# New byte offsets for the FFN hidden tiles and for the mixers' view of the normed activations in an fp32 two-part matmul kernel

## The reference, cut to what matters

```python
# first block, each of 2 layers; second block alike, with three attention branches and no cross attention
h = h + 0.5 * swiglu_ffn(rms_norm(h, ffn1_norm[l]), ffn1_w_in[l], ffn1_w_out[l])   # up 1024 -> 2 x 2816, down 2816 -> 1024
h = h + hybrid_mixer(rms_norm(h, mix_norm[l]), w_in[l], ..., w_out[l])
h = h + memory_cross_attention(rms_norm(h, xattn_norm[l]), rms_norm(mem, mem_norm[l]), w_q, w_kv, w_o)
h = h + 0.5 * swiglu_ffn(rms_norm(h, ffn2_norm[l]), ffn2_w_in[l], ffn2_w_out[l])

def swiglu(h, w_in, w_out):
    g, u = split(h @ w_in, 2)
    return (silu(g) * u) @ w_out
```

## Time and profile before

| what | value |
|---|---|
| median of 3 runs | 2719.12 us (2718.63, 2719.12, 2724.09) |
| the profiled execution | 2723.83 us |
| its span, first to last instruction | 2721.8 us |
| instructions in the profile | 39409 |
| TensorE matmul busy | 2666.2 us, 98% of the span |
| VectorE, ScalarE, GpSimd busy | 56%, 50%, 9% |
| mean granted TensorE clock | 0.990 |
| HBM traffic | 156 GB/s over the span |

### The profile page before, as it was taken

One profiled execution on the slowest core, in us unless ns is written; L12 is line 12 of the kernel. 1 busy time (PEld: TensorE's weight loads), 2 busy tenths in 40 slices (PEclk: granted clock), 3 DMA queues, 4 the chain that ended last, 5 costly groups with the idle time before them and its releaser, 6 DMA issues.

```text
span 2721.8 us, 39409 instructions
## 1 busy us (share of the span) xinstructions
PE 2666.2 (98%) x14932; PEld 2275.9 (84%) x14932; DVE 1525.2 (56%) x2103; ACT 1365.0 (50%) x2147; POOL 256.3 (9%) x155
## 2 busy tenths in 40 slices
PE   8999999999999999999999999999999999999998
PEld 6889987888888898787888879888888888878887
DVE  5557635465555774455555546467555555557654
ACT  5447335454544562555445445555445444455543
POOL 0100201000000002200100000443000000245000
PEclk9999998999999999999999999999999999999999
DMA  6555213355555541146855554325555555324654
GB/s 246 186 178 172 90 47 102 131 183 185 197 185 187 169 147 48 62 155 161 214 186 182 186 187 151 108 94 173 188 184 183 185 186 169 125 92 136 201 186 136
DMA packets 117803, 427.54 MB, mean 157 GB/s; under 512 B 13004, under 2 KB 14796, under 8 KB 117132
## 3 DMA queue, kind: packets, MB, share of 16 engines
q1 hardware_dynamic: 117152, 424.59, 47.8%
q10 hardware_dynamic: 492, 0.69, 0.1%
HBM read 423.79 MB, written 1.44 MB: 156 GB/s over the span
## 4 chain that ended last, share of the span: by engine, by line
PE 92%; DVE 3%; ACT 3%; issue 1%; DMA 1%; POOL 0%; SPq 0%; ACTq 0%; DVEq 0%
PE bank L460 75%; PE bank L1621 2%; PE bank L964 2%; PE bank L480 2%; PE bank L656 1%; PE bank L1668 1%; PE bank L1637 1%; PE bank L602 1%; PE bank L1124 1%; PE bank L1135 1%; ACT hi_slots L434 1%; PE bank L1133 1%; DVE lo_slots L448 1%; DMA raw<-w_full 1%; PE bank L1651 0%
## 5 line engine op out<-in xcount | busy, mean ns | idle before, releaser
L448 DVE TENSOR_TENSOR lo_slots<-raw,hi_slots 128x1024 fp32r<-128x1024 f32 x732 | 899.6, 1234 | 770.1 <-ACT hi_slots L434 769.6
L434 ACT ACTIVATE hi_slots<-raw 128x1024 fp32r<-128x1024 f32 x788 | 830.1, 1057 | 671.1 <-PE bank L460 660.2
L460 PE MATMUL bank<-hi_slots,x_hi 128*128 128x512 f32 x1600 | 634.3, 396 | 4.4 <-DVE lo_slots L425 4.0
L460 PE MATMUL bank<-hi_slots,x_lo 128*128 128x512 f32 x1600 | 624.2, 390 | 0.0
L460 PE MATMUL bank<-lo_slots,x_hi 128*128 128x512 f32 x1600 | 623.6, 390 | 0.0
L460 PEld LDWEIGHTS bank<-hi_slots,x_hi 128*128 128x128 f32 x1600 | 301.1, 188 | 66.9 <-DVE lo_slots L425 4.8
L460 PEld LDWEIGHTS bank<-hi_slots,x_lo 128*128 128x128 f32 x1600 | 300.8, 188 | 64.0
L460 PEld LDWEIGHTS bank<-lo_slots,x_hi 128*128 128x128 f32 x1600 | 301.3, 188 | 59.0
L460 PE MATMUL bank<-x_hi,hi_slots 128*128 128x256 f32 x1152 | 332.2, 288 | 1.3 <-ACT bias_mem L975 0.8
L460 PE MATMUL bank<-x_lo,hi_slots 128*128 128x256 f32 x1152 | 326.1, 283 | 0.0
L460 PE MATMUL bank<-x_hi,lo_slots 128*128 128x256 f32 x1152 | 326.0, 283 | 0.0
(11 more groups left out here) (310 smaller groups left out, 3070.4 us busy)
## 6 DMA issues: line engine op xcount, KB each, us to landing
raw<-w_full SPq DMA_DIRECT2D x792, 512.0 KB, 3.3
bias_mem<-bias_rows SPq DMA_DIRECT2D x8, 288.0 KB, 7.2
mem<-mem_t SPq DMA_DIRECT2D x2, 1024.0 KB, 7.8
const<-consts SPq DMA_DIRECT2D x1, 1664.0 KB, 7.1
h<-x_t SPq DMA_DIRECT2D x1, 1024.0 KB, 5.2
final<-finals SPq DMA_DIRECT2D x2, 512.0 KB, 7.3
out_t<-h SPq DMA_DIRECT2D x4, 256.0 KB, 2.3
bias_rows<-junk ACTq DMA_DIRECT2D x1, 384.0 KB
```

The lines of the kernel that those rows point to most:

```text
L434: nc.scalar.activation(w_hi[s], raw[s][:, :], ACT.Copy).then_inc(hi_ready[s], 1)
L448: nc.vector.tensor_tensor(w_lo[s], raw[s][:, :], w_hi[s].bitcast(F32), ALU.subtract).then_inc(lo_ready[s], 1)
L460: mm = nc.tensor.matmul(out, lhsT=a, rhs=b, start=start and n == 0, stop=stop and n == len(passes) - 1)
```

## The change

`x_hi` and `x_lo` become rooms that are 16 floats (64 bytes) longer. Each room has two views: `x_hi`/`x_lo` begin 64 bytes in, `xm_hi`/`xm_lo` at its start. Where the normed activations are for a mixer or the cross attention, ScalarE and VectorE write them through the `xm` views and TensorE reads them through these; FFNs and output projections keep `x_hi`/`x_lo`. `hid_pad` shrinks from 32 to 16 floats. `param`, `small`, `seam_gain`, `junk` and the pads are put in another order. Worked out as above, the starts modulo 2048 after the change are: `hi_slots`, `lo_slots`, `h` 128 as before; `x_hi`, `x_lo` 128 as before, though at other addresses (`x_hi` from byte 59520 to 77952, `x_lo` from 67712 to 100480); `xm_hi`, `xm_lo` 64; `hid_hi`, `hid_lo`, `hid`, `xs` 128 instead of 192; `const` 128 instead of 64; `mem_hi`, `mem_lo`, `y_hi`, `y_lo` 64 as before. The number of instructions, their order and their waits stay.

```diff
+SHIFT = 16
         h = sb("h", [P, TT, D_MODEL])
-        x_hi = sb("x_hi", [P, KT, TOK], F32R)
-        x_lo = sb("x_lo", [P, KT, TOK], F32R)
-        junk = sb("junk", [P, HALF])
-        mem_pad = sb("mem_pad", [P, 496])
+        param = sb("param", [P, N_PARAM])
+        small = sb("small", [P, 16])
...
+        mem_pad = sb("mem_pad", [P, 24])
...
+        x_hi_room = sb("x_hi_room", [P, KT * TOK + SHIFT], F32R)
         const = sb("const", [P, N_CONST])
-        param = sb("param", [P, N_PARAM])
         ab_now_hi = sb("ab_now_hi", [P, KT * 8], F32R)
+        x_pad = sb("x_pad", [P, 48])
+        x_lo_room = sb("x_lo_room", [P, KT * TOK + SHIFT], F32R)
+        x_hi, x_lo = (room[:, SHIFT:].rearrange("p (k t) -> p k t", k=KT) for room in (x_hi_room, x_lo_room))
+        xm_hi, xm_lo = (room[:, 0:KT * TOK].rearrange("p (k t) -> p k t", k=KT) for room in (x_hi_room, x_lo_room))
...
-        hid_pad = sb("hid_pad", [P, 32], F32, ffn_mem)
+        hid_pad = sb("hid_pad", [P, SHIFT], F32, ffn_mem)
         hid_hi = sb("hid_hi", [P, FT, TOK], F32R, ffn_mem)
...
-        def act_turned(normed, hf, banks, gain):
+        def act_turned(normed, hf, banks, gain, to=x_hi):
...
-                nc.scalar.activation(x_hi[:, k, :], turned(banks, k), ACT.Copy,
+                nc.scalar.activation(to[:, k, :], turned(banks, k), ACT.Copy,
...
-            pe_lead(E, group, ev, x_hi, x_lo, lambda k: pe.wait_ge(*x_ready(normed, k)), rest)
+            pe_lead(E, group, ev, xm_hi, xm_lo, lambda k: pe.wait_ge(*x_ready(normed, k)), rest)
...
-            feature_block(u % SLOTS, x_hi, x_lo, bank[2 + g % 2][:, 0:TOK]).then_inc(block_done[u % SLOTS], 1)
+            feature_block(u % SLOTS, xm_hi, xm_lo, bank[2 + g % 2][:, 0:TOK]).then_inc(block_done[u % SLOTS], 1)
...
```

More of the change, by code:

```diff
@@ L250, in build @@
         h = sb("h", [P, TT, D_MODEL])
-        x_hi = sb("x_hi", [P, KT, TOK], F32R)
-        x_lo = sb("x_lo", [P, KT, TOK], F32R)
-        junk = sb("junk", [P, HALF])
-        mem_pad = sb("mem_pad", [P, 496])
+        param = sb("param", [P, N_PARAM])
+        small = sb("small", [P, 16])
+        eps_col, mean_part = small[:, 0:4], small[:, 8:8 + TT]
+        squares = small[:, 4:8].rearrange("p (a t) -> p a t", a=2)
+        rstd, rstd_first = small[:, 10:10 + TT], small[:, 12:12 + TT]
+        seam_gain = sb("seam_gain", [P, KT])
+        mem_pad = sb("mem_pad", [P, 24])
         raw_mem = ExitStack()
@@ L273, in build @@
         mem_sum, mem_rstd = (bias_mem[:, at_norm + n * TOK:at_norm + (n + 1) * TOK] for n in range(2))
[L274 to L279, removed]
+        junk = sb("junk", [P, HALF])
+        stage_pad = sb("stage_pad", [P, 432])
         ffn_mem, mix1, cross, mix2 = ExitStack(), ExitStack(), ExitStack(), ExitStack()
-        hid_pad = sb("hid_pad", [P, 32], F32, ffn_mem)
+        hid_pad = sb("hid_pad", [P, SHIFT], F32, ffn_mem)
         hid_hi = sb("hid_hi", [P, FT, TOK], F32R, ffn_mem)
@@ L621, in pe_turn_scaled, with dve_turned @@
                         mm.then_inc(sems["xt_ps"], 1)
-        def act_turned(normed, hf, banks, gain):
+        def act_turned(normed, hf, banks, gain, to=x_hi):
             for k in range(4 * hf, 4 * hf + 4):
                 act.wait_ge(sems["xt_ps"], normed * 4 + k // 2 + 1)
-                nc.scalar.activation(x_hi[:, k, :], turned(banks, k), ACT.Copy,
+                nc.scalar.activation(to[:, k, :], turned(banks, k), ACT.Copy,
                                      scale=gain[:, k:k + 1]).then_inc(sems["xhi_ready"], 1)
-        def dve_turned(normed, hf, banks, gain, part=(0, 4)):
+        def dve_turned(normed, hf, banks, gain, part=(0, 4), to=(x_hi, x_lo)):
             for k in range(4 * hf + part[0], 4 * hf + part[1]):
                 dve.wait_ge(sems["xhi_ready"], normed * KT + (k | 1) + 1)
-                nc.vector.scalar_tensor_tensor(out=x_lo[:, k, :], in0=turned(banks, k), scalar=gain[:, k:k + 1],
-                                               in1=x_hi[:, k, :].bitcast(F32), op0=ALU.mult,
+                nc.vector.scalar_tensor_tensor(out=to[1][:, k, :], in0=turned(banks, k), scalar=gain[:, k:k + 1],
+                                               in1=to[0][:, k, :].bitcast(F32), op0=ALU.mult,
                                                op1=ALU.subtract).then_inc(sems["xlo_ready"], 1)
@@ L896, in pe_mix1_project @@
             pe.wait_ge(sems["ab_lo"], E.after("ab_lo", 1))
-            three(bank[4][0:8, 0:TOK], [(ab_now_hi[:, k * 8:k * 8 + 8], ab_now_lo[:, k * 8:k * 8 + 8], x_hi[:, k, :],
-                                         x_lo[:, k, :]) for k in range(KT)]).then_inc(sems["ab_ps"], 1)
-            pe_section(E, 1, 1, 3, x_hi, x_lo)
+            three(bank[4][0:8, 0:TOK], [(ab_now_hi[:, k * 8:k * 8 + 8], ab_now_lo[:, k * 8:k * 8 + 8], xm_hi[:, k, :],
+                                         xm_lo[:, k, :]) for k in range(KT)]).then_inc(sems["ab_ps"], 1)
+            pe_section(E, 1, 1, 3, xm_hi, xm_lo)
         def act_mix1_project(E):
@@ L1054, in pe_gdn @@
         def pe_gdn(E):
-            pe_group(E, 4, 4, 0, x_hi, x_lo)
+            pe_group(E, 4, 4, 0, xm_hi, xm_lo)
             pe.wait_ge(sems["ab_sb"], E.after("ab_sb", 1))
@@ L1066, in pe_gdn @@
             mm.then_inc(sems["gdn_ss"], 1)
-            pe_group(E, 5, 5, 0, x_hi, x_lo)
+            pe_group(E, 5, 5, 0, xm_hi, xm_lo)
             for i in range(4):
@@ L1081, in pe_gdn @@
                 mm.then_inc(sems["gdn_bc"], 1)
-            pe_token_pair(E, 6, 6, 0, x_hi, x_lo)
+            pe_token_pair(E, 6, 6, 0, xm_hi, xm_lo)
             pe.wait_ge(sems["gate_dve"], E.after("gate_dve", 4))
@@ L1108, in pe_gdn @@
                 pe_gate_rows(G_BETA, t, bank[4], c("ident")).then_inc(sems["row_ps"], 1)
-                pe_token_pair(E, 6, 6, 2, x_hi, x_lo, (t,), [bank[2][:, tile_cut(n)] for n in range(TT)])
+                pe_token_pair(E, 6, 6, 2, xm_hi, xm_lo, (t,), [bank[2][:, tile_cut(n)] for n in range(TT)])
                 pe.wait_ge(sems["kv_scaled"], E.after("kv_scaled", 3 * t + 3))
@@ L1802, in pe_cross @@
             pe_normed(E, 2, 13, 7, lambda: pe.wait_ge(sems["mem_ev"], E.after("mem_ev", MEM_EVACS)))
-            pe_section(E, 14, 8, 1, x_hi, x_lo)
+            pe_section(E, 14, 8, 1, xm_hi, xm_lo)
             for s in range(SLOTS):
@@ L1825, in pe_mix2_project @@
                 for s in range(2 if g in (1, 4) else SLOTS):
-                    pe_block(E, E.mid(g, s), s, g, x_hi, x_lo)
+                    pe_block(E, E.mid(g, s), s, g, xm_hi, xm_lo)
                 if g in (1, 4):
-                    pe_token_pair(E, g, g, 2, x_hi, x_lo)
+                    pe_token_pair(E, g, g, 2, xm_hi, xm_lo)
                 if g == 2:
@@ L2054, in act_full @@
             for hf in range(2):
-                act_turned(normed, hf, turns, gain)
+                act_turned(normed, hf, turns, gain, xm_hi)
         def dve_full(E, n, state, normed, turns, gain):
@@ L2059, in dve_full @@
             for hf in range(2):
-                dve_turned(normed, hf, turns, gain)
+                dve_turned(normed, hf, turns, gain, to=(xm_hi, xm_lo))
         def act_ffn_ended(E, state, u):
@@ L2215, in _ @@
                         for hf in range(2):
-                            act_turned(E.normed(1), hf, FFN_TURNS, gain(E, "mix", 0, KT))
+                            act_turned(E.normed(1), hf, FFN_TURNS, gain(E, "mix", 0, KT), xm_hi)
                         act_mem_key(E, 1)
@@ L2240, in _ @@
                         for hf in range(2):
-                            act_turned(E.normed(2), hf, STICK_TURNS, p1(E, "xattn", 0, KT))
+                            act_turned(E.normed(2), hf, STICK_TURNS, p1(E, "xattn", 0, KT), xm_hi)
                         act_mem_values(E, 3)
@@ L2323, in _ @@
                         split_lo(E, FFN_UNITS - 1)
-                        dve_turned(E.normed(1), 0, FFN_TURNS, gain(E, "mix", 0, KT))
+                        dve_turned(E.normed(1), 0, FFN_TURNS, gain(E, "mix", 0, KT), to=(xm_hi, xm_lo))
                         dve_mem_unit(E, 0)
-                        dve_turned(E.normed(1), 1, FFN_TURNS, gain(E, "mix", 0, KT))
+                        dve_turned(E.normed(1), 1, FFN_TURNS, gain(E, "mix", 0, KT), to=(xm_hi, xm_lo))
                         dve_mem_unit(E, 1)
@@ L2344, in _ @@
                         for hf in range(2):
-                            dve_turned(E.normed(2), hf, STICK_TURNS, p1(E, "xattn", 0, KT))
+                            dve_turned(E.normed(2), hf, STICK_TURNS, p1(E, "xattn", 0, KT), to=(xm_hi, xm_lo))
                         for j in range(2, MEM_KEPT):
```

## The result

| | median | runs |
|---|---|---|
| before | 2718.88 us | 4 (2718.21 to 2724.09) |
| changed | 2695.18 us | 4 (2693.01 to 2700.3) |

The ratio is 0.9911, 95% interval 0.9893 to 0.993: 24 us faster. The forecast of 2689 is a ratio of 0.989; it lies just outside the first interval and inside the second, and both medians lie in the range.

What follows compares the result with a forecast made beforehand. TensorE, busy 98% of the span, was taken to bound the kernel through the distance between matmul starts. The gains, 13.3 + 17.6 + 0.8 - 1.7 = 30.0 us, off the 2719.1 us median gave 2689, range 2678 to 2704.

Steps and rivals of the forecast that it cites:

- (1): FFN down half: hid moved from 192 to 128 cuts 233.4 to 227.1 ns over 2112 matmuls, 13.3 us gained.
- (2): Mixers: x streamed from 64 goes from 120 to a mean 114.9 ns over 3456 matmuls, 17.6 us gained.
- A: Rival: all streamed x blocks settle at the longer distance, 118.0 ns; 19.8 us gained, 2699 us; chance 0.15.
- B: Rival: all streamed x blocks settle at the shorter distance, 113.3 ns; 37.0 us gained, 2682 us; chance 0.17.
- (3): token_pair, stationary operand now at 64: 120.0 to 117.9 ns over 376 matmuls, 0.8 us gained.
- (4): Transposes, with const, hid and xs moved to 128: costed at nothing, with up to 4.9 us either way.
- (5): Given back through late operands in the delta rule's part, token pairs and half-clock starts: 1.7 us in all.
- The cover: In the projection, weight reload and split (5.6 us) were to finish before the slot's next use (10.9 to 11.3 us).
- Rival C: Only one edit works, or late VectorE or ScalarE takes back about half of (2): 2698 to 2706 us; chance 0.08.
- D: Rival: the two distances belong to the stages, not the tiles, so nothing changes, 2719 us; chance 0.03.
- E: Rival: coarser address bits matter, so moved x_hi and x_lo slow the FFN's up half; 17 us slower, 2736; chance 0.03.

Runs made afterwards that it cites:

- kernel of the mixers alone: The changed kernel with the hid pad back at 32 floats (hid at 192, mixers' x streamed from 64): 2706.99 us, ratio 0.994 to the kernel before.
- e9_restarts: The changed kernel with const back at 64 modulo 256, the small tile hid at 192, ab_now_hi shifted too: 2694.14 us, ratio 0.9892 to the kernel before.

## Why the prediction was right

The direction, the mechanism and the range held, and the steps, each by its own measure, are:

- **(1) `hid`:** 13.3 us foreseen, 13.8 measured in the traces, 11.8 as a time by itself. The up half was the right row to take it from.
- **(2) `x` streamed:** 17.6 foreseen with the mix of the `y` blocks (114.9 ns), 18.3 measured (114.6). 2413 of some 3400 steps in the trace are at the short distance, close to the 8 in 12 of `y`. The two distances were foreseen rightly; that the mix came so near was luck. Six of the eight short `y` blocks are one unbroken run, and in the changed kernel it fell into the long distance, which left 3 in 12 short. With `x` at the same offset the mean was 115.3 in the kernel of the mixers alone and 115.6 in e9_restarts. Rivals A and B, all blocks at one distance, didn't come: long streams took the short one, every other gate the long one.
- **(3) token pair:** 0.8 foreseen, 1.4 measured. 138 of some 370 steps were at the short distance, which L964, the row it was taken from, shows in 22 of 351.
- **(4) `const` and the transposes at nothing:** this step failed. The streams behind the transposes got slower: 2.1 us in the up half, 1.1 us in the `y` blocks, and both went back when e9_restarts moved `const` and `hid` back. I had looked at the length of the transposes and not at what follows them. The 5 us that I had set beside (4) covered it in size.
- **(5) given back:** 1.7 us foreseen, 3.9 in new waits. The cover failed at one place, the first mixer's projection (a wait for `lo_slots`, 1.6 us); and where attention begins TensorE waits another 2.3 us, because a small VectorE operation now falls behind the start of a GpSimd one; the forecast had no term for that. The cover was reckoned with 5.6 us for a reload and its split, from the median landing of 3.3 us and without other work in between. At the place of the wait it took 14.9 us, more than the 10.9 to 11.3 us after which a slot is used again.

So the parts came to 33.5 us where 31.7 was foreseen, and 7.1 was lost where 1.7 was: 26 in place of 30. The wait of TensorE for a split is the one that the forecast said should not appear.

One reading of the forecast was too short. It says that the mean duration doesn't show the difference, from the first of three forms (396 ns for either tile). The other two forms had 390 ns with `x` and 394 with `hid`, and with `hid` at 128 its three have 391, 389 and 389. The durations hint at the effect, and give less than its size.

Rival C (one edit without effect) fell with the two single edits, D (nothing to do with the tiles) with `hid` at ten offsets and the FFN's `x` at 64. E asked for coarser address bits: `x_hi` and `x_lo` moved by 18 and 32 KB and the up half's steady distance stayed at 227. The forecast read the rule of the Trainium skill (SBUF — State Buffer, "Who interferes with whom"), two independent read ports and a TensorE that never waits, as leaving no room for an effect of offsets. Read so, it doesn't hold in these traces: with the same matmuls in the same order, the distance was between 226.9 and 234.3 ns by where the stationary tile began. Whether the two ports are independent no run here shows. The Trainium skill (TensorE: Matmul & The Clock Gate, "Wait — 56ns, not 53.3ns?") gives 215.7 ns from start to start for back-to-back matmuls of 512 columns at the full clock; the lowest resting distance of these fp32r streams was 226.8.

What stays open: why 256 bytes, whether the distance from the weights or the tile's own address counts, what inside the chip makes the two resting distances, and what picks one. The runs show where they occur and no more.

## What to carry to other kernels

Where TensorE bounds a kernel and the streams are long, work out the step from start to start for every form of matmul, and compare forms that differ only in the address of one operand; a pad of 64 bytes was worth 12 us here and a second view of one tile 16. Try each role by itself, in steps of 64 bytes over 256, for the best offset of the stationary tile (128 here, with the streamed weights at 128) is not the best of the streamed tile (64 here, with the stationary weights at 128). After moving anything, read again the streams whose addresses did not change: they can settle on another distance. And judge an offset of a streamed tile by all its streams, for one long stream shows one of two distances.

## What the runs showed that I had not expected

- The pattern returns every 256 bytes for `hid` (54.96 us at 64 and 320, 54.45 at 128 and 384, 56.01 at 256 and 512), and for `x` in the one pair tried (57.42 at 64 and 320).
- The two sides differ: against 128, `hid` at 64 costs 2.1 ns a matmul, at 192 6.5.
- For `hid` the offsets off the 64-byte steps were never good: 96, 160 and 224 gave 233.4, 233.3 and 234.3 ns.
- A stream can settle on either of two distances, and what is changed elsewhere shifts the choice: 144 `y` matmuls and what follows them took 36.75 or 37.39 us by where `const` stood, with `y` and the weights in place.
- A cover reckoned from a median can fail at one place: 14.9 us for a load and its split, where 5.6 was reckoned.
- A VectorE operation on one element per partition took 0.15 us, or 2.29 us where it began 0.10 us behind a GpSimd subtraction; with the faster streams their order turned round.
